# Start of a two-layer decoder kernel: scaling x ahead of rounding weights, six adaLN tiles on the sync queue, a weight pair between last tile and sum

## The reference, cut to what matters

```
mod = silu(c) @ ada_w[i] + ada_b[i]            # 2048 -> 6 * 2048
sh_mix, sc_mix, g_mix, sh_mlp, sc_mlp, g_mlp = split(mod)
h = rmsnorm(x, norm_mix[i]) * (1 + sc_mix) + sh_mix
proj = h @ w_in                                # q, k, v and 16 forget logits
```

## Time and profile before

| | |
|---|---|
| median of three runs | 2415.48 us |
| the profiled execution's own time | 2407.41 us |
| its span | 2405.5 us |
| PE busy | 2321.5 us (97%) |
| DVE busy | 1631.0 us (68%) |
| ACT busy | 1051.2 us (44%) |
| POOL busy | 220.3 us (9%) |
| mean DMA rate | 256 GB/s |

### The profile page before, as it was taken

One profiled execution on the slowest core, in us unless ns is written; L12 is line 12 of the kernel. 1 busy time (PEld: TensorE's weight loads), 2 busy tenths in 40 slices (PEclk: granted clock), 3 DMA queues, 4 the chain that ended last, 5 costly groups with the idle time before them and its releaser, 6 DMA issues.

```text
span 2405.5 us, 29055 instructions
## 1 busy us (share of the span) xinstructions
PE 2321.5 (97%) x11331; PEld 1954.3 (81%) x11331; DVE 1631.0 (68%) x1539; ACT 1051.2 (44%) x1183; POOL 220.3 (9%) x402
## 2 busy tenths in 40 slices
PE   3999999998999999999998999998999999999998
PEld 3989899777888888888886888876888888888886
DVE  3768788777776776775775888855786555455455
ACT  3254343445434434434445444434543443443453
POOL 4401111010100100100110111100010000000000
PEclk9899999999999999999998999999999999999999
DMA  8978789676986986986984898854796655655563
GB/s 303 365 264 275 276 316 368 225 289 209 319 288 225 324 284 227 321 288 227 320 290 157 306 349 320 316 177 154 265 319 208 197 187 191 193 191 185 192 203 122
DMA packets 262337, 615.61 MB, mean 256 GB/s; under 512 B 14704, under 2 KB 15040, under 8 KB 261312
## 3 DMA queue, kind: packets, MB, share of 16 engines
q1 hardware_dynamic: 203072, 403.73, 49.5%
q0 software_dynamic: 55296, 201.35, 23.5%
q10 hardware_dynamic: 3840, 8.68, 1.0%
HBM read 611.62 MB, written 2.10 MB: 255 GB/s over the span
## 4 chain that ended last, share of the span: by engine, by line
PE 93%; DVE 3%; ACT 2%; issue 1%; DMA 1%; POOL 0%; ACTq 0%; DVEq 0%; POOLq 0%
PE ps L447 26%; PE ps L449 26%; PE ps L448 26%; PE ps L434 3%; PE ps L435 2%; PE ps L436 2%; PE ps L726 1%; PE ps L521 1%; PE ps L487 1%; PE ps L484 1%; ACT w_hi L796 1%; DMA raw<-in_fox_w_in_dram 1%; DVE w_lo L1193 1%; DMA start_ring<-in_ada_w_dram 0%; PE ps L646 0%
## 5 line engine op out<-in xcount | busy, mean ns | idle before, releaser
L1193 DVE TENSOR_TENSOR w_lo<-raw,w_hi 128x1024 fp32r<-128x1024 f32 x740 | 903.4, 1224 | 615.9 <-ACT w_hi L796 613.6
L796 ACT ACTIVATE w_hi<-raw 128x1024 fp32r<-128x1024 f32 x740 | 783.5, 1060 | 1141.9 <-PE ps L449 1055.0
L447 PE MATMUL ps<-w_hi,h 128*128 128x512 f32 x1536 | 611.9, 398 | 6.5 <-DVE h L1306 6.5
L449 PE MATMUL ps<-w_lo,h 128*128 128x512 f32 x1536 | 604.3, 393 | 0.0
L448 PE MATMUL ps<-w_hi,h 128*128 128x512 f32 x1536 | 604.0, 393 | 0.0
L447 PE MATMUL ps<-w_hi,mid 128*128 128x512 f32 x1280 | 503.5, 393 | 2.6 <-DVE mid L1699 2.6
L449 PE MATMUL ps<-w_lo,mid 128*128 128x512 f32 x1280 | 499.8, 390 | 0.0
L448 PE MATMUL ps<-w_hi,mid 128*128 128x512 f32 x1280 | 499.3, 390 | 0.0
L447 PEld LDWEIGHTS ps<-w_hi,h 128*128 128x128 f32 x1536 | 292.8, 191 | 69.2 <-issue 9.3
L449 PEld LDWEIGHTS ps<-w_lo,h 128*128 128x128 f32 x1536 | 292.1, 190 | 62.5
L448 PEld LDWEIGHTS ps<-w_hi,h 128*128 128x128 f32 x1536 | 292.9, 191 | 59.5 <-issue 0.5
(11 more groups left out here) (202 smaller groups left out, 1297.4 us busy)
## 6 DMA issues: line engine op xcount, KB each, us to landing
ada_raw<-in_ada_w_dram POOLq DMA_DIRECT2D x320, 512.0 KB, 6.4
raw<-in_mlp_w_up_dram SPq DMA_DIRECT2D x128, 1024.0 KB, 5.4
raw<-in_mlp_w_down_dram SPq DMA_DIRECT2D x128, 1024.0 KB, 6.3
raw<-in_fox_w_in_dram SPq DMA_DIRECT2D x48, 1024.0 KB, 9.1
raw<-in_conv_w_in_dram SPq DMA_DIRECT2D x48, 1024.0 KB, 7.6
start_ring<-in_ada_w_dram POOLq DMA_DIRECT2D x64, 512.0 KB, 8.6
raw<-in_fox_w_out_dram SPq DMA_DIRECT2D x16, 1024.0 KB, 8.4
raw<-in_conv_w_out_dram SPq DMA_DIRECT2D x16, 1024.0 KB, 5.2
```

Of the source, the lines that this page charges most:

```text
L447: mm(o, xh, hi, start=(k == 0), stop=False)
L449: last = mm(o, xh, lo, start=False, stop=(k == KC - 1))
L796: op(w_hi[:, e % WR], raw[:, e // 2, EK * (e % 2):EK * (e % 2 + 1)], ACT.Copy).then_inc(hi_ready, 1)
L1193: v.tensor_tensor(w_lo[:, e % WR], raw[:, e // 2, EK * (e % 2):EK * (e % 2 + 1)], w_hi[:, e % WR].bitcast(F32), ALU.subtract).then_inc(spl ...
```

## The change

There are three edits, all in the start stage.

1. ScalarE no longer rounds the two halves of `raw` 0 right after the root of the statistics; `start_split(0)` and `start_split(1)` now stand behind all `scale_x` and `copy_x` and the rounding of the forget weights.
2. Tiles 0 to 5 are issued by SP, right behind the transfer of c and ahead of all `raw` quarters, on semaphores of their own (`start_first`). POOL issues tiles 6 to 31 behind its constants. The shapes of the transfers are the same; what the readers wait for is changed accordingly.
3. TensorE's order in groups 1 to 3: behind `start_pair(n + 2)` stood forget logits, tile 5, pair n + 3, tile 7, sum. Now there stand tile 5, forget logits, tile 7, pair n + 3, sum.

```diff
--- before.py
+++ after.py
@@ -195,6 +195,7 @@
         vec_arrived = sem("vec_arrived")
         x_arrived = sem("x_arrived")
         wf_arrived = sem("wf_arrived")
+        start_first = [sem(f"start_first{i}") for i in range(RING)]
         start_arrived = [sem(f"start_arrived{i}") for i in range(RING)]
         raw_arrived = [sem(f"raw_arrived{i}") for i in range(NQ)]
         ada_arrived = [sem(f"ada_arrived{i}") for i in range(TILES)]
@@ -309,6 +310,9 @@
             layer, part = PARTS[b]
             return ada_w[layer][P * k:P * (k + 1), D * part + NA * n:D * part + NA * (n + 1)]
 
+        def start_tile_of(t, b):
+            return ada_w[0].rearrange("(k p) n -> p k n", p=P)[:, 2 * (t % 8):2 * (t % 8) + 2, ds(D * b + NU * (t // 8), NU)]
+
         def cols(n):
             return slice(NU * n, NU * (n + 1))
 
@@ -334,6 +338,10 @@
                 for q in range(NQ):
                     sp.wait_ge(split_ready, NE * (u - 1) + 2 * q + 2)
                     sp.dma_start(raw[:, q], quarter(w, row0, q, col)).then_inc(raw_arrived[q], 16)
+
+            for t in range(RING):
+                for b in range(2):
+                    sp.dma_start(start_ring[:, t, :, b, :], start_tile_of(t, b)).then_inc(start_first[t], 16)
 
 
             for i in range(3 * NQ):
@@ -369,17 +377,11 @@
         @block.gpsimd
         def _(pool):
             def start_load(t):
-                m, r = t // 8, t % 8
-                if t >= RING:
-                    pool.wait_ge(start_steps, START_STEPS[t - RING + 1])
-                    pool.wait_ge(start_used, (t - RING + 1) // 2)
+                pool.wait_ge(start_steps, START_STEPS[t - RING + 1])
+                pool.wait_ge(start_used, (t - RING + 1) // 2)
                 for b in range(2):
-                    pool.dma_start(start_ring[:, t % RING, :, b, :],
-                                   ada_w[0].rearrange("(k p) n -> p k n", p=P)[:, 2 * r:2 * r + 2, ds(D * b + NU * m, NU)]
-                                   ).then_inc(start_arrived[t % RING], 16)
-
-            for t in range(2):
-                start_load(t)
+                    pool.dma_start(start_ring[:, t % RING, :, b, :], start_tile_of(t, b)).then_inc(start_arrived[t % RING], 16)
+
             pool.memset(ident[:, :], 0.0).then_inc(const_ready, 1)
             pool.memset(ident_r[:, :].bitcast(F32), 0.0).then_inc(const_ready, 1)
             pool.memset(causal[:, :].bitcast(F32), 0.0).then_inc(const_ready, 1)
@@ -391,8 +393,6 @@
             for m in (ident, ident_r):
                 pool.affine_select(out=m[:, :], in_=m[:, :].bitcast(F32), compare_op=ALU.not_equal, fill=1.0,
                                    base=0, pattern=[[-1, P]], channel_multiplier=1).then_inc(const_ready, 1)
-            start_load(2)
-            start_load(3)
 
             for i in range(2):
                 pool.wait_ge(const_ready, 9 + i)
@@ -403,7 +403,7 @@
             for a in range(TT):
                 pool.affine_select(out=upto[:, a, :], in_=upto[:, a, :], compare_op=ALU.is_ge, fill=0.0,
                                    base=-P * a, pattern=[[1, T]], channel_multiplier=-1).then_inc(const_ready, 1)
-            for t in range(4, START_TILES):
+            for t in range(RING, START_TILES):
                 start_load(t)
 
 
@@ -513,7 +513,7 @@
                 t = 8 * m + r
                 if r == 1 and m:
                     pe.wait_ge(start_mod, m)
-                pe.wait_ge(start_arrived[t % RING], 32 * (t // RING + 1))
+                pe.wait_ge(*((start_first[t], 32) if t < RING else (start_arrived[t % RING], 32 * (t // RING))))
                 k = 2 * r + 1
                 for b in range(2):
                     for j in range(NB):
@@ -607,10 +607,10 @@
                 start_pair(n + 1)
                 start_tile(m, 3)
                 start_pair(n + 2)
+                start_tile(m, 5)
                 forget_logits(m - 1)
-                start_tile(m, 5)
+                start_tile(m, 7)
                 start_pair(n + 3)
-                start_tile(m, 7)
                 start_sum(m)
             n = 6 * (NG - 1)
             start_pair(n - 2)
@@ -854,9 +854,6 @@
                 for a in range(TT):
                     square(0, n, a)
             take_root(0, 0)
-            start_split(0)
-            start_split(1)
-
             def scale_x(m):
                 act.wait_ge(inv_ready, TT)
                 if m >= 2:
@@ -901,9 +898,8 @@
                 high(0, e)
 
             for m in range(NG - 1):
-                if m:
-                    start_split(6 * m)
-                    start_split(6 * m + 1)
+                start_split(6 * m)
+                start_split(6 * m + 1)
                 start_pair(2 * m)
                 start_pair(2 * m + 1)
                 for i in range(2, 6):
@@ -1280,7 +1276,7 @@
                     dve.wait_ge(x_turned, NG)
                 if r == 0 and m >= 2:
                     dve.wait_ge(start_summed, m - 1)
-                dve.wait_ge(start_arrived[t % RING], 32 * (t // RING + 1))
+                dve.wait_ge(*((start_first[t], 32) if t < RING else (start_arrived[t % RING], 32 * (t // RING))))
                 for kk in range(2 - r % 2):
                     k = 2 * r + kk
                     ada_step(k, start_accs[m % 2], start_ring[:, t % RING, kk, :, :], k, start_steps, START_STEPS[t] + kk)
```

## The result

The changed kernel is faster: ratio to the kernel before, run on the same chip, 0.9947 with the 95% interval 0.9925 to 0.997, which is 12.8 us off 2415.5 (7 to 18). The medians of the four runs of each are 2396.43 and 2413.93 us, further apart than the ratio says; with so few runs the interval is what counts. A second series among the experiments gave 0.9958 (0.9944 to 0.9971), 10.1 us. The forecast of 9.2 us lies in both intervals.

A forecast was written before the change was run, and what follows sets the result against it. TensorE was taken to bound the kernel, its start delayed by scaling queued behind `raw` 0's rounding. Terms 6.5 (step 48), 1.3 (lag) and 1.4 (clock) gave 9.2 us off, 2406.3 us; range 2399.5 to 2412.5.

The forecast's parts named there:

- What bounds the start: First 60 us: scaling of x queued behind the rounding waiting for `raw` 0; freeing it gains at most 15.9 us.
- SP's tiles cost 7 us at `inv`: Start stage: with tiles on SP's queue, `inv` comes near 36 instead of 28.89 and x is turned from 37.5.
- the walk through the bytes: Start stage: estimate of queues sharing DMA packet by packet; tile 4 lands near 32, `inv` near 36, 8.8 us gained.
- SP's issues are out by 6.6 us: Start of SP's queue: 12 issues of about 0.41 us each, all out by about 6.6 us.
- 13.8 us from turn to sum: Start stage: 13.8 us of TensorE from turning x to first sum, ending near 51.3; DVE's 15th step gains 8.8 us.
- 2.5 us given back by `raw` 2: Asked for at step 15: `raw` 2 meets a full queue, takes 11.4 us instead of 8.9; sign: 11 us or more.
- the byte total: Up to `raw` 8 and the last tile: 45.4 MB at 0.38 MB/us ends at 122.5, allowing at most about 12 us.
- The pair: Around the last sum: a pair between last tile and sum gains 1.3 to 1.5 us of lag and 1.4 of clock.
- Nothing takes it back after 165 us: After the start stage: the lead is carried to the end, with no new TensorE gap after 165 us.
- B: Start stage: tiles come nearly in the old time, `inv` by 31; 14 us off, 2401.5 us; chance 22%.
- C: Later `raw` turns: bandwidth takes the lead back, 2.5 us left at step 48; 4 off, 2411.5 us; chance 27%.
- D: Start stage: SP's queue starves, tile 4 lands after 41 us (near 46 gives 2420.5 us); kernel slower; chance 6%.

The follow-up runs named there:

- after_again: The changed kernel with all three edits, unaltered, run and traced a second time beside the kernel before: ratio 0.9958 (0.9944 to 0.9971).
- e4_again: Edits 1 and 3, without edit 2, on the kernel before, second run: ratio 0.9932 (0.9912 to 0.9953).
- e6_pool_held: The changed kernel with POOL also waiting for tile 4's steps before asking for tile 6; ratio to the kernel before 0.9935 (0.9912 to 0.9957).
- e1: Edit 1 (ScalarE's order) alone on the kernel before: ratio 0.9946 (0.9926 to 0.9966).
- e4_scale_pair: Edits 1 and 3, without edit 2, on the kernel before, first run: ratio 0.9942 (0.9921 to 0.9963).
- e4_third: Edits 1 and 3, without edit 2, on the kernel before, third run: ratio 0.9941 (0.9922 to 0.9960).
- e4: The kernel before with edits 1 and 3, without edit 2, run three times: ratios 0.9942, 0.9932 and 0.9941.
- e2: Edit 2 (SP issuing tiles 0 to 5) alone on the kernel before: ratio 1.0009 (0.9992 to 1.0026).
- e3: Edit 3 (TensorE's order) alone on the kernel before: ratio 0.9989 (0.9971 to 1.0008).

## Why the prediction was right, point by point

- **What bounds the start.** Right: the scaling was queued behind the rounding of `raw` 0. Edit 1 alone gives 0.9946. That SP's tiles and the new order leave it at 0.9947 fits the signs of the steps: one costs (6.3 us between after_again and e4_again), one gives (1 to 4 us). The rounding of `raw` 0 came 16.4 us behind the first scaling, not "some 9", and its second half ended at 54.4, when the first sum did: it was hidden, with nothing to spare.
- **SP's tiles cost 7 us at `inv`.** Right, by the walk through the bytes: forecast 36, x turned from 37.5; measured 35.84 and 37.51. Its parts were rougher than that: tile 4 forecast near 32, landed at 31.74, but tile 5 near 37, landed at 34.8; tile 1 near 14, landed at 10.0; x near 15, landed at 18.4. Only tile 4 decided `inv`. DMA queues (packets, MB, share of 16 engines) in 12:14 and 20:22 of the changed kernel:

```profile
q10 hardware_dynamic: 80, 0.66, 78.9%
q1 hardware_dynamic: 80, 0.16, 21.7%
...
q0 software_dynamic: 140, 0.51, 67.7%
q1 hardware_dynamic: 131, 0.24, 32.8%
```

  80 packets against 80, 0.66 MB of x against 0.16 of tiles; then 140 against 131, 0.51 MB of POOL's against 0.24. e6_pool_held shows it: take POOL's packets away and `inv` is back at 28.2. The Trainium skill ("DMA: Bandwidth & Descriptors", Issuing engines are not separate DMA queues) has the transfers of all engines interleave on the same 16 DMA engines, and the trace agrees. It adds that starting them from several engines saves only the sequencer's time. Here the measurement differs: asked for by SP, tile 4 landed 6.9 us later (24.8 before, 31.7 after).
- **SP's issues are out by 6.6 us.** Wrong, and without harm. The tenth took 2.0 us, the eleventh 6.7 and the twelfth 3.5 (SP's timeline; the first row covers two):

```profile
8.41 10.27 SPq L344 DMA_DIRECT2D start_ring<-in_ada_w_dram  x2
...
15.18 3.50 SPq L344 DMA_DIRECT2D start_ring<-in_ada_w_dram  x1
```

  The last was out at 18.68. Tile 3 was still under way then (it landed at 26.2), so tile 5 was hardly later for it; that is argued, no run shows it.
- **13.8 us from turn to sum.** Too short: 16.9. This is the term that was mis-sized; it came from one trace in which the clock happened to rise within the chain. In 6 of 14 traces it did (13.8), in the 8 others not (16.7 to 16.9). So the gain at step 15 was 5.7 us and not 8.8, and the first sum ended at 54.4, past the 53 that the prediction had named as its sign.
- **2.5 us given back by `raw` 2.** Wrong: it took 5.0 us, and "11 us or more" was another of the prediction's signs. The DMA engines were full while it flowed (share 1.02 from 57.15 to 62.20), but POOL's queue had little left in it: from 59.3 on it moved 0.29 MB against 0.87 of SP's. POOL's requests at 43.2 and 49.9 had waited for TensorE's tiles among the slow turns. Nor was `raw` 2 on the path: though it was 3.9 us quicker than before, the lead of 5.7 us at step 15 is the same at step 24. What was given back came at `raw` 3, 13.0 us against 11.8: DVE's 27th step ends at 87.2, 91.7 before. In all 0.8 us was given back to step 48: gain 4.9 against a forecast of 6.5 (6.3 by its own terms, rounded up without a reason), inside the bounds of 1 to 12 (6.6 in the second trace). With edit 1 and without SP's tiles the gain at step 48 is 11.1 to 12.1 in three traces (e1, e4_scale_pair and e4_third), at the 12 that the byte total was said to allow, and 8.9 in e4_again, where the clock rose late.
- **The pair.** TensorE's lag: forecast 1.3 to be won, measured 1.3 in the first trace (4.9 at step 48, 6.2 at `start_store`). The reason given for it does not hold: TensorE was to stand for 2 or 3 us ahead of the last sum, but it was busy for all of 130 to 141 us. In the second trace TensorE was 2.6 us behind DVE's last step, and 1.1 us was lost instead (6.6 at step 48, 5.5 at `start_store`). The clock: forecast the half of 2.9, measured 2.9 in the first trace and 2.8 in the second: it stayed high.
- **Sum.** 6.5 + 1.3 + 1.4 = 9.2 forecast; 4.9 + 1.3 + 2.9 = 9.1 at the mark in the first trace, 6.6 - 1.1 + 2.8 = 8.3 in the second. The agreement of the sums is luck: two terms were off by about 1.5 in opposite directions.
- **Nothing takes it back after 165 us.** Wrong for the profiled execution, as the last section shows, and not to be seen in the ratios, which give 12.8 and 10.1 us.
- **Rivals.** B (tiles in the old time) is out for this kernel but is what e6_pool_held and e4 realise: 14 us less than 2415.5 are the 2401.5 given for it. C (the lead is taken back by the time of step 48, to within 3 us of 143.7) is out: step 48 came at 138.8 and 137.2. So is its form in which all leads come down to one: leads at the mark run from -5.3 to +15.3. D is out; its mechanism is the right one, but tile 4 landed 6.9 us later than before, and D needed 16 or more (41 us).

The version that beats both kernels is edits 1 and 3 without 2: 0.9932 to 0.9942 in three series, 14 to 16 us off. Against the changed kernel its mark is 4 to 7 us earlier (4.8 side by side), and its time was lower by 6.3 us in the one series that had both, which the overlapping intervals leave likely and not certain; e6_pool_held, which keeps edit 2 with the extra wait, is as good (0.9935).

## What to carry to other kernels

Look at what stands behind a wait in an engine's queue: work whose operands had been there for 14 us stood behind a rounding that waited for a transfer, and moving it was worth 13 us (e1), while asking for the transfers earlier was worth nothing (e2). When transfers are shifted from one queue to another on a full DMA, count packets: queues take turns by packet, so the queue with 2 KB packets, 0.70 MB in 2 us when alone, got 0.24 beside one of 3.6 KB and 0.16 beside one of 8 KB. And give a chain a duration from more than one trace if the clock can rise within it.

## What the runs showed that was not expected

**Half clock late in the execution moves with the start.** From 230 us on the lead of 9.1 us shrank to 3.1 at 400 us and 2.9 at the end. The places, in the changed kernel and then in the kernel before:

```profile
235.00:246.00 11.00, 11.00 (x34) 8.60 (x34) 0.32 (x1) 0.00 (x0) 0.53 (x1) 0.53 0.66 248
...
320.00:335.00 15.00, 15.00 (x56) 11.70 (x55) 4.40 (x4) 1.06 (x1) 1.59 (x3) 0.66 0.73 274
```

```profile
235.00:246.00 11.00, 11.00 (x57) 8.87 (x55) 8.93 (x8) 4.10 (x4) 2.12 (x4) 0.97 1.03 387
...
320.00:335.00 15.00, 15.00 (x86) 12.44 (x84) 11.91 (x11) 5.05 (x5) 2.64 (x5) 1.00 1.01 371
```

Clock 0.53 and 0.66 of full where before had 0.97 and 1.00. Before had its own low stretch at 245 to 252, so 1.5 us were lost there, and 4.5 us at 324 to 334. Both traces of the changed kernel have these, and the trace of e4_again has shorter ones at the same places, while e1, e3 and the other two of e4 lack the second. Summed from 170 us on to the last ten, half clock lasts 38 to 75 us in the traces, and 14 us more of it cost 6.2. The instructions behind the start are the same in all; what differs is when they come. The two profiles of the changed kernel show only 3.1 and 2.5 us of the gain; they are the slowest of four and the second slowest of twelve executions, while the profiled execution of before was faster than all three of its timed ones. The timed runs point the same way. Of 34 executions of the kernel before on one chip the six fastest took 2400.5 us in the mean at a mean granted clock of 0.985, the six slowest 2416.0 at 0.979; 0.006 of the execution is 29 us of half clock, which at 6.2 per 14 would be 13 of these 15.5 us, an estimate. So the clock goes along with most of the scatter; that it alone makes it was not tested.

**Narrow products did not raise the clock.** 105 products of 128 columns with the identity, without a gap for some 25 us, left it low; three of 512 float32 columns (recorded as six) ended with the clock at full after 5.5 us, in the one trace that there is. Width, data (an identity is mostly zeros) and type differ between the two, so which of them matters stays open.
